# The order of TensorE's work in the delta rule: one place per level for the weight products, and the sums behind weight products

## What is computed

```
def step(S, inp):
    r_t, w_t, k_t, v_t, kk_t, a_t = inp
    sa = jnp.einsum('bhvk,bhk->bhv', S, kk_t)
    S = (S * w_t[:, :, None, :]
         - jnp.einsum('bhv,bhk->bhvk', sa, kk_t * a_t)
         + jnp.einsum('bhv,bhk->bhvk', v_t, k_t))
    return S, jnp.einsum('bhvk,bhk->bhv', S, r_t)
...
y_rw = _head_norm(y_rw, RWKV_LN_EPS).reshape(B, T, RWKV_WIDTH) * lnx_w + lnx_b
bonus = (jnp.sum(rh * kh * r_k, axis=-1, keepdims=True) * vh).reshape(B, T, RWKV_WIDTH)
out_rw = (y_rw + bonus) * gate
```

## Time and profile before

| | before |
|---|---|
| median of three runs | 2444.94 us |
| profiled execution | 2444.8 us |
| its span | 2443.1 us |
| TensorE (PE) busy | 2397.3 us, 98% of the span |
| VectorE (DVE) busy | 1408.0 us, 58% |
| ScalarE (ACT) busy | 1133.7 us, 46% |
| GpSimd (POOL) busy | 239.2 us, 10% |
| mean granted TensorE clock | 0.996 |
| the eight passes of the delta rule | from 179.78 us to about 580 us |

### The profile page before, as it was taken

How to read it: one execution, slowest core, us unless ns; L and a number is a source line. 1 busy time by engine, 2 the same in 40 slices (tenths; PEclk the granted TensorE clock), 3 DMA queues, 4 the chain that set the end, 5 groups by cost and what they waited for, 6 DMA issues and landing times.

```text
span 2443.1 us, 32012 instructions
## 1 busy us (share of the span) xinstructions
PE 2397.3 (98%) x11646; PEld 2016.5 (83%) x11646; DVE 1408.0 (58%) x1629; ACT 1133.7 (46%) x1459; POOL 239.2 (10%) x184
## 2 busy tenths in 40 slices
PE   7999999999999999999999999989999999999998
PEld 6878888888788888888888888878888888888886
DVE  5467777776555545545555566775555555555554
ACT  5454444444444344344344445764543443443443
POOL 0001123342000000000000000230000000000001
PEclk9999999999999999999999999999999999999999
DMA  7642232333565665665665665545666666656654
GB/s 220 189 148 86 83 90 85 88 87 98 172 187 182 196 191 181 195 191 181 195 187 186 187 199 173 180 149 187 182 190 193 187 189 192 188 187 193 189 188 157
DMA packets 215414, 410.92 MB, mean 168 GB/s; under 512 B 13264, under 2 KB 19792, under 8 KB 215184
## 3 DMA queue, kind: packets, MB, share of 16 engines
q1 hardware_dynamic: 213888, 407.01, 54.2%
q0 software_dynamic: 1424, 2.49, 0.4%
HBM read 407.35 MB, written 2.10 MB: 168 GB/s over the span
## 4 chain that ended last, share of the span: by engine, by line
PE 87%; DVE 2%; ACT 2%; issue 0%; POOL 0%; ACTq 0%; DVEq 0%; POOLq 0%
PE acc L209 25%; PE acc L211 25%; PE acc L210 25%; PE tp_pair L692 6%; PE tp_pair L306 2%; PE acc L692 2%; PE acc L1494 1%; PE tp_pair L1494 1%; DVE stg L639 1%; ACT w_hi L193 0%; ACT L684 0%; DVE w_lo L198 0%; DVE state L864 0%; DVE gate_t L1557 0%; DVE stg L640 0%
## 5 line engine op out<-in xcount | busy, mean ns | idle before, releaser
L198 DVE TENSOR_TENSOR w_lo<-raw,w_hi 128x1024 fp32r<-128x1024 f32 (+1 forms) x760 | 988.5, 1306 | 888.7 <-ACT w_hi L193 886.9
L193 ACT ACTIVATE w_hi<-raw 128x1024 fp32r<-128x1024 f32 (+1 forms) x760 | 801.5, 1057 | 940.9 <-PE acc L211 928.3
L209 PE MATMUL acc<-w_hi,xT_hi 128*128 128x512 f32 (+1 forms) x1760 | 706.1, 401 | 4.9 <-DVE w_lo L198 4.3
L211 PE MATMUL acc<-w_hi,xT_lo 128*128 128x512 f32 (+1 forms) x1760 | 684.2, 389 | 0.0
L210 PE MATMUL acc<-w_lo,xT_hi 128*128 128x512 f32 (+1 forms) x1760 | 683.1, 388 | 0.0
L211 PEld LDWEIGHTS acc<-w_hi,xT_lo 128*128 128x128 f32 x1760 | 330.9, 188 | 68.6
L209 PEld LDWEIGHTS acc<-w_hi,xT_hi 128*128 128x128 f32 x1760 | 331.8, 188 | 66.6 <-DVE xT_lo L366 3.8
L210 PEld LDWEIGHTS acc<-w_lo,xT_hi 128*128 128x128 f32 x1760 | 331.9, 189 | 60.7
L209 PE MATMUL acc<-w_hi,hidA_hi 128*128 128x512 f32 x640 | 252.2, 394 | 6.3 <-DVE hidA_lo L1528 6.3
L209 PE MATMUL acc<-w_hi,hidB_hi 128*128 128x512 f32 x640 | 250.6, 392 | 0.0
L210 PE MATMUL acc<-w_lo,hidA_hi 128*128 128x512 f32 x640 | 250.5, 391 | 0.0
(11 more groups left out here) (228 smaller groups left out, 1714.7 us busy)
## 6 DMA issues: line engine op xcount, KB each, us to landing
raw<-in_ff_w SPq DMA_DIRECT2D x512, 512.0 KB, 3.7
raw<-in_ev_w_in SPq DMA_DIRECT2D x112, 512.0 KB, 3.6
raw<-in_od_w_in SPq DMA_DIRECT2D x64, 512.0 KB, 4.3
raw<-in_ev_w_out SPq DMA_DIRECT2D x32, 512.0 KB, 3.8
raw<-in_od_w_out SPq DMA_DIRECT2D x32, 512.0 KB, 3.8
raw<-in_ev_w_in SPq DMA_DIRECT2D x8, 288.0 KB, 6.0
x<-in_x_in SPq DMA_DIRECT2D x4, 512.0 KB, 7.7
gate_w<-in_gx_w SPq DMA_DIRECT2D x8, 256.0 KB, 2.7
```

The source lines that it names most:

```text
L193: act.activation(w_hi[:, j % RING, :, 0:wide], raw[:, j % RING, :, 0:wide], ACT.Copy).then_inc(hi_ready, 1)
L198: dve.tensor_tensor(w_lo[:, j % RING, :, 0:wide], raw[:, j % RING, :, 0:wide], w_hi[:, j % RING, :, 0:wide], ALU.subtract).then_inc(lo_rea ...
L209: nc.tensor.matmul(o, hi[:, tok], wh, start=(kt == 0), stop=False)
L211: last = nc.tensor.matmul(o, lo[:, tok], wh, start=False, stop=(kt == KT - 1))
```

## The change

In `rwkv_pe`, TensorE's list for a pass is put in another order. No instruction is added or taken away, and no other engine's list is touched.

- Head: `pe_variance` moves ahead of the key transposes, directly behind the first three parts. The two parts behind the variance leave this place, so that nothing stands between the key transposes and the beta transposes.
- `pe_front_lora` moves ahead of the inverse's start transposes, directly behind two parts. Two parts now stand behind those transposes.
- Levels: the part ahead of `y` goes, and three parts stand behind `y` in place of two. The front sum moves from the end of level 3 to behind the three parts of level 4, ahead of the update.
- The number of parts ahead of each level's update is 10, 13, 16, 19 and 22 in both orders. Ahead of `y` it is 8, 11, 14, 17 and 20 before, and 7, 10, 13, 16 and 19 after.

```
             more(pe, p, parts, 3)
+            if norm:
+                pe_variance(pe, p - 1)
             pe.wait_ge(sem("tokens_ready"), 3 * p + 1)
             for c in range(NCHUNK):
                 last = nc.tensor.transpose(tp[0][:, c * P:(c + 1) * P], key_bd[:, c, :], ident)
             last.then_inc(sem("tokens_done"), 1)
-            if norm:
-                pe_variance(pe, p - 1)
-            more(pe, p, parts, 2)
             pe.wait_ge(sem("seen_ready"), 5 * p + 5)
             for c in range(NCHUNK):
                 last = nc.tensor.transpose(tp[3][:, c * P:(c + 1) * P], beta_bd[:, c, :], ident)
             last.then_inc(sem("tokens_done"), 1)
             more(pe, p, parts, 2)
+            if front:
+                pe_front_lora(pe, p + 1)
             pe.wait_ge(sem("inv_start"), p + 1)
             for c in range(NCHUNK):
                 last = nc.tensor.transpose(tp[1][:, c * P:(c + 1) * P], key_bd[:, c, :], ident)
             last.then_inc(sem("inv_t_done"), 1)
-            if front:
-                pe_front_lora(pe, p + 1)
+            more(pe, p, parts, 2)
             pe.wait_ge(sem("tokens_ready"), 3 * p + 2)
             for l in range(1, LEVELS):
-                more(pe, p, parts, 1)
                 pe.wait_ge(sem("level_ready"), 5 * p + l)
                 pe.wait_ge(sem("inv_t_ready"), LEVELS * p + l)
                 for c in range(NCHUNK):
                     last = mm(tp[2][:, c * P:(c + 1) * P], level_a[:, c, :], inv_t[:, c, :])
                 last.then_inc(sem("y_done"), 1)
-                more(pe, p, parts, 2)
+                more(pe, p, parts, 3)
+                if l == 4 and front:
+                    pe_front_sum(pe, p + 1)
                 pe.wait_ge(sem("w_ready"), 5 * p + l)
                 if l > 1:
                     pe.wait_ge(sem("inv_ready"), 4 * p + l - 1)
...
-                if l == 3 and front:
-                    pe_front_sum(pe, p + 1)
```

## The result

The changed kernel takes 2452.45 us, the median of seven runs (2451.82 to 2454.04), against 2444.94 us for the seven of the kernel before (2443.4 to 2445.38): 7.5 us more, a ratio of 1.0031 with a 95% interval of 1.0022 to 1.0041. The profiled execution took 2451.82 us with a span of 2450.1, 7.0 us more than the span before.

A forecast was written before the change was run, and what follows sets the result against it. TensorE, busy for 98% of the span, was taken to bound the kernel. Terms of 5.0 + 4.2 - 0.3 = 8.9 us on 2444.8 gave 2453.7 us, 0.36% slower, with a range from 2447 to 2459 us.

The forecast's parts named there:

- TensorE is full, so an order pays only by waits: TensorE's delta-rule passes: order matters only through idle time removed or made and the cost of switching between kinds of matmul.
- a change of kind costs nothing: Levels: switching between delta matmuls and weight products is free in sum; eight small matmuls and six products take 2.27 us.
- The rival on it: Product runs in each pass: switching kinds does cost, so fewer runs save 6.0 us in all, 2447.7 us; chance 0.12.
- The head, +5.0 us: Passes 1 to 6: beta transposes wait for VectorE's last mask, 0.83 us a pass, +5.0 us in all.
- The levels, +4.2 us: Levels 2 to 5, eight passes: `y` waits for ScalarE's copy of the inverse, 0.13 us each, +4.2 us.
- estimate that each bared wait exposes a whole load: `y` in levels 2 to 5: by the skill page, (0.06 + 0.107) x 32 = 5.3 us in place of 4.2.
- Pass 7, -0.3 us: Last pass: two parts ahead of the first `y` remove its wait for the copy, 0.25 + 0.07 us, -0.3 us.
- Pass 0's head, 0: First pass: held by VectorE, then GpSimd's mask; taking LoRA matmuls ahead fills idle time that stays in sum, 0.
- The rest: Elsewhere: the update never waits, GpSimd's masks are in time, and no later stage gives the loss back; no cost.
- the signs: Expected traces: beta transposes idle about 0.8 us, pass about 51.7 us, small `y` idle times from ScalarE's copy, update never waiting.
- `y` is free: Levels: the copy is in time or starting from idle costs nothing, leaving 4.7 us, so 2449.5 us; chance 0.15.
- a long wait at `y`: Levels: `y` waits as long as in pass 7, 0.32 us each, +14.9 us in total, 2459.7 us; chance 0.10.

The follow-up runs named there:

- the levels alone: Kernel before with its head order kept, three parts behind `y` in each level and the front sum in level 4: 2449.0 us against 2445.23, ratio 1.0016.

## Why the prediction was right

- *TensorE is full, so an order pays only by waits.* Borne out by all traces. The term "a change of kind costs nothing" was the boldest, since the first product of a run looks 0.09 us dearer. The rival on it (2447.7 us) fell in three traces: with five runs of products fewer a pass got longer, with four more it stayed (50.45), and the one product ahead of `y` gained.
- *The head, +5.0 us.* The trace has 0.72 in pass 1 and 0.8 in passes 2 to 6, 4.8 together, and 0.59 us of idle time where about 0.77 was forecast. The idle time is counted from the modelled end of the last transposes. Counted as in the prediction, 1.73 us behind the start of the variance (388.33), TensorE was free at 390.06 and waited until 390.82: 0.76. From start to start the 0.83 is met by 0.82. The start of the beta transposes, 0.48 us behind the mask's start by pass 0, came 0.46 behind.
- *The levels, +4.2 us.* Mechanism right, size off. Passes 1 to 6 lose 0.27 us each (0.20 in the table up to the fifth `y`, 0.07 at it), not 0.52: 1.6 us. Passes 0 and 7 lose 0.4 and 0.3, near the 0.5 forecast. Together 2.3. The term that was mis-sized is the delay behind ScalarE's copy: 0.15 us, read from pass 7 alone, which is written out. In the looped passes it is 0.10, so that `y` comes 0.01 us late and only the start from idle, 0.06 us, is left of the 0.13. With the loop written out the delay was 0.14 and a level 4.87 to 4.88 us, 0.12 to 0.13 more than the 4.75 of before. The Trainium skill (TensorE: Matmul & The Clock Gate, LDWEIGHTS (loading the stationary operand)) gives the weight load as columns / 1.2 ns, 107 ns for 128 columns. The prediction's estimate that each bared wait exposes a whole load isn't borne out: the start from idle cost 0.06 us here.
- *Pass 7, -0.3 us.* Its head is 0.24 shorter for the same work, and its first `y`, now covered, gives the rest; with the head alone changed, the whole pass is 0.35 shorter.
- *Pass 0's head, 0.* It takes 10.46 us up to `y` where it took 10.47: the 0.67 us that TensorE waited ahead of the inverse's transposes are gone, and its wait ahead of `y` grew from 0.79 to 1.65.
- *The rest.* The update waits nowhere, GpSimd's masks are in time with the rotations ahead of them, and no later stage gives anything back: 4.8 + 2.3 - 0.2 = 6.9 of the span's 7.0 us. Of the signs, one didn't show: the list of waits puts no idle time down to ScalarE's copy. The pass was forecast at about 51.7 us and is 51.5, by the mis-sized term.
- *The other rivals.* "`y` is free" (2449.5) is ruled out by the levels alone, 50.77 us a pass; a long wait at `y` (2459.7) by levels of 4.81 us.

## What to carry to other kernels

Where one engine is full, its busy share won't tell what a new order does; make a list of what each block waits for, with the time at which that is ready and the time at which the block gets there, and the difference is the price. Filler work is worth its length wherever it fills a wait and nothing elsewhere; in this kernel a run of products more costs about 0.01 us, so filler is best cut small and laid only where there is a wait. When a wait is bared, look at what the late engine does just before: here the masks stood behind work that nobody needed yet.

## What was not expected of the hardware

- A wait in TensorE's hardware loop let `y` start 0.10 us behind ScalarE's copy, the same wait written out 0.14 to 0.15 us behind it. The beta transposes' wait for VectorE's mask shows no such difference: they start 0.05 to 0.06 us behind the mask's end in looped and in written-out passes alike (pass 0 against passes 1 to 6 of the change, and passes 1 to 6 written out). So it isn't the loop as such. `y` has two waits ahead of it and the beta transposes one; whether this is the reason was not tried.
- In the trace of the levels alone, TensorE's granted clock falls in pass 0, to 0.50 (1.2 of 2.4 GHz), and `y` holds TensorE for 1.7 us (189.62 to 191.32) in place of 0.88. Ahead of it TensorE had been idle for 1.30, 1.14 and 0.67 us. The change has idle times of 1.31, 1.14 and 1.65 us there and kept the clock at 1.00 in its profile. In the traces with the masks ahead of the mix and with two products ahead of the fourth chunk's wait the clock fell some microseconds earlier, to a mean of 0.70 and 0.74 from 175 to 180 us, and pass 0 began at 181.7 and 181.9 us in place of 179.2 to 180.3. The levels alone have a pass 0 that is 0.9 us longer than the change's. So a single profile of this kernel can carry one to two microseconds that belong to the clock and not to the edit (an estimate from these rows); the looped passes, at 1.00 in all, are the better measure. One row of each, the levels alone and then the change:

```profile
189.50:191.00 1.50, 1.38 (x6) 1.41 (x7) 1.10 (x1) 0.00 (x0) 0.02 (x1) 0.50 0.86 235
```

```profile
189.50:191.00 1.50, 0.89 (x9) 0.92 (x9) 1.50 (x1) 0.00 (x0) 0.51 (x1) 1.00 0.57 89
```
